# The normaliser sums of an mLSTM block with the keys as the moving operand, in column groups of TensorE

## The reference, cut to what matters

```python
def step(carry, inp):                       # _mlstm_chunked, float32
    C, n, m = carry
    ...
    wsL = jnp.exp(bL[..., None] - b + ib - m_new[..., None])
    wpL = jnp.exp(bL + m - m_new)
    C_new = wpL[..., None, None] * C + jnp.einsum('bhs,bhsv,bhsd->bhvd', wsL, vb, kb)
    n_new = wpL[..., None] * n + jnp.einsum('bhs,bhsd->bhd', wsL, kb)
    return (C_new, n_new, m_new), h
```

## Time and profile before

| | |
|---|---|
| runs, median (lowest to highest) | 2135.77 us (2133.35 to 2139.61) |
| the profiled execution, its own time | 2138.1 us |
| its span | 2136.3 us |
| TensorE busy | 2047.6 us, 96% |
| VectorE, ScalarE, GpSimd busy | 49%, 20%, 42% |
| mean granted TensorE clock | 0.979 of full |
| moved by DMA | 224.49 MB, 105 GB/s |

### The profile page before, as it was taken

How to read it: one execution, slowest core, us unless ns; L and a number is a source line. 1 busy time by engine, 2 the same in 40 slices (tenths; PEclk the granted TensorE clock), 3 DMA queues, 4 the chain that set the end, 5 groups by cost and what they waited for, 6 DMA issues and landing times.

```text
span 2136.3 us, 33690 instructions
## 1 busy us (share of the span) xinstructions
PE 2047.6 (96%) x13453; PEld 1871.6 (88%) x13453; DVE 1047.9 (49%) x1230; ACT 428.8 (20%) x671; POOL 895.3 (42%) x568
## 2 busy tenths in 40 slices
PE   6999999899999999989999999999899999999997
PEld 5989988799999999989998746547499999999996
DVE  4655646554415414576962356555732441442345
ACT  3232333321101100131212323323211110010011
POOL 4323333145445445554553123223445444544543
PEclk9999999899999999999999999999999999999998
DMA  4122212122222222233232474756732222222222
GB/s 174 60 70 78 85 54 91 42 69 70 78 79 70 79 79 70 88 108 127 79 103 77 144 259 146 275 191 208 282 104 74 71 76 79 69 79 72 76 79 89
DMA packets 82080, 224.49 MB, mean 105 GB/s; under 512 B 6352, under 2 KB 11344, under 8 KB 81232
## 3 DMA queue, kind: packets, MB, share of 16 engines
q1 hardware_dynamic: 73344, 202.94, 28.7%
q10 hardware_dynamic: 8656, 20.39, 2.6%
HBM read 170.06 MB, written 53.25 MB: 105 GB/s over the span
## 4 chain that ended last, share of the span: by engine, by line
PE 85%; DVE 8%; DMA 3%; ACT 2%; issue 1%; POOL 1%; DVEq 0%; SPq 0%; ACTq 0%; POOLq 0%
PE psd L211 12%; PE psd L216 11%; PE psd L212 11%; PE psd L215 11%; PE psd L217 11%; PE psd L218 11%; PE psm L429 2%; PE psm L1397 1%; PE psd L1293 1%; DMA c_s<-CsB 1%; PE psd L1282 1%; PE psd L1219 1%; DMA CsB<-st_c 1%; PE psm L1382 1%; DVE ntmp L306 1%
## 5 line engine op out<-in xcount | busy, mean ns | idle before, releaser
L1986 POOL CAST whi<-wraw 128x1024 fp32r<-128x1024 f32 x223 | 236.7, 1062 | 935.2 <-PE psd L218 501.9
L1988 POOL TENSOR_TENSOR wlo<-wraw,whi 128x1024 fp32r<-128x1024 f32 x223 | 543.9, 2439 | 17.9
L211 PE MATMUL psd<-xh,whi 128*128 128x320 f32 x896 | 286.3, 320 | 9.6 <-ACT xh L269 3.5
L215 PE MATMUL psd<-xl,whi 128*128 128x320 f32 x896 | 279.6, 312 | 2.7 <-POOL xl L324 2.2
L211 PE MATMUL psd<-ah,whi 128*128 128x320 f32 x864 | 269.2, 312 | 12.1 <-DVE ffs L974 7.7
L212 PE MATMUL psd<-xh,whi 128*128 128x320 f32 x896 | 278.8, 311 | 0.0
L216 PE MATMUL psd<-xl,whi 128*128 128x320 f32 x896 | 278.7, 311 | 0.0
L218 PE MATMUL psd<-xh,wlo 128*128 128x320 f32 x896 | 278.6, 311 | 0.0
L217 PE MATMUL psd<-xh,wlo 128*128 128x320 f32 x896 | 278.6, 311 | 0.0
L212 PE MATMUL psd<-ah,whi 128*128 128x320 f32 x864 | 267.9, 310 | 0.0
L216 PE MATMUL psd<-al,whi 128*128 128x320 f32 x864 | 267.8, 310 | 0.0
(11 more groups left out here) (396 smaller groups left out, 3225.2 us busy)
## 6 DMA issues: line engine op xcount, KB each, us to landing
wraw<-w SPq DMA_DIRECT2D x224, 512.0 KB, 3.5
CsA<-st_c SPq DMA_DIRECT2D x7, 1024.0 KB, 6.3
CsB<-st_c SPq DMA_DIRECT2D x7, 1024.0 KB, 9.1
c_s<-CsA SPq DMA_DIRECT2D x7, 1024.0 KB, 6.5
c_s<-CsB SPq DMA_DIRECT2D x7, 1024.0 KB, 9.4
ztp<-st_c SPq DMA_DIRECT2D x5, 1024.0 KB, 8.4
CsC<-st_c SPq DMA_DIRECT2D x5, 1024.0 KB, 9.4
c_s<-ztp SPq DMA_DIRECT2D x5, 1024.0 KB, 4.2
```

The costliest lines, as they stand in the source:

```text
L211: pe.matmul(o0, wh, x0, start=st, stop=False)
L215: pe.matmul(o0, wh, l0, start=False, stop=False)
L1986: pool.tensor_copy(whi[s][:], wraw[s][:]).then_inc(w_high, 1)
L1988: pool.tensor_tensor(wlo[s][:], wraw[s][:], whi[s][:].bitcast(F32), ALU.subtract).then_inc(w_split, 1)
```

## The change

For each head the sums are made in three steps. First, in column groups: for each of the four prompt tiles one product with a 128x32 block `n_one` as the stationary operand (a column of ones, the rest zeros) and the tile of keys, 512 columns, as the moving one; the four write to four groups of 32 partitions of bank 1, so that partitions 0, 32, 64 and 96 hold the four partial sums. A fifth product with `n_smp` (columns 1 to 8 pick the streams) adds the streams' sums to partitions 1 to 8. They are issued ahead of the products L1377 and L1379. Second, ScalarE copies the bank to a new tile `nrow` (step "nr"). Third, after L1377 and L1379, four products take 128 columns of `nrow` each as the stationary operand and 16 columns `n_sum` as the moving one, which turns the sums onto the partitions of the key and adds the four partial sums up. VectorE reads them at a stride of 16 columns. The three constants are put in places of the parameter tile that the convolution has used up, by four more operations of `fold`, for which the gate products wait.

```diff
+        NW = 16
+        n_one, n_smp = [par[:, PAR["convw"] + GW * i:PAR["convw"] + GW * (i + 1)] for i in range(2)]
+        n_sum = par[:, PAR["convb"]:PAR["convb"] + NW]
...
+        nrow = sb("nrow", [P, SEQ], at=x3)
...
-                                  + {0: ["nu"], 2: ["sum", ("upd", 0)], 4: [("upd", 1)], 6: ["var", ("upd", 2)],
+                                  + {0: ["nr", "nu"], 2: ["sum", ("upd", 0)], 4: [("upd", 1)], 6: ["var", ("upd", 2)],
...
-                               + [("num", f) for f in kts] + ["dn", "dnS", "D", "DS", ("Cp", 0)]
+                               + [("num", f) for f in kts] + ["dn", "nr", "dnS", "D", "DS", ("Cp", 0)]
...
+                link(v.memset(par[:, PAR["convw"]:PAR["convw"] + 2 * GW], 0.0))
+                link(v.memset(n_one[:, 0:1], 1.0))
+                link(v.tensor_copy(n_smp[:, 1:1 + NB], con[:, CON["ind"]:CON["ind"] + NB]))
+                link(v.tensor_copy(n_sum, gsel[:, 0:NW]))
...
-                pe.wait_ge(self.gw, 30)
+                pe.wait_ge(self.gw, 34)
...
             def pe_normalisers(self, pe, h):
 
                 P_, V_, S_ = self.P, self.V, self.S
+                for c in range(NP):
+                    mm = pe.matmul(bank[1][GW * c:GW * (c + 1), :], n_one, ktok[:, c, :], start=True, stop=c > 0,
+                                   skip_group_check=True)
+                mm = pe.matmul(bank[1][0:GW, :], n_smp, ktok[:, NP, :], start=False, stop=True, skip_group_check=True)
+                mm.then_inc(P_.sem, 1)
                 pe.wait_ge(V_.sem, V_.at("qn", h))
                 pe.matmul(bank[0][:, 0:P], ones, att[:, tt(NP)], start=True, stop=False)
                 for k in range(KH):
                     pe.matmul(bank[0][:, 0:P], ones, rt[:, k, :], start=False, stop=(k == KH - 1))
+                pe.wait_ge(S_.sem, S_.at("nr", h))
                 for k in range(KH):
-                    for c in range(NP):
-                        pe.matmul(bank[0][:, P + k:P + k + 1], ktok[:, c, tt(k)], ones[:, 0:1], start=(c == 0),
-                                  stop=(c == NP - 1))
-                    mm = pe.matmul(bank[0][:, 2 * P + NB * k:2 * P + NB * (k + 1)], ktok[:, NP, tt(k)],
-                                   con[:, CON["ind"]:CON["ind"] + NB], start=True, stop=True)
+                    mm = pe.matmul(bank[0][:, P + NW * k:P + NW * (k + 1)], nrow[:, tt(k)], n_sum, start=False,
+                                   stop=(k == KH - 1), skip_group_check=True)
                 mm.then_inc(P_.sem, 1)
...
-                    v.tensor_copy(nP[:, h, :], bank[0][:, P:P + KH]).then_inc(V_.sem, 1)
+                    both = bank[0][:, P:P + NW * KH].rearrange("p (k b) -> p k b", b=NW)
+                    v.tensor_copy(nP[:, h, :].unsqueeze(2), both[:, :, 0:1]).then_inc(V_.sem, 1)
                     v.wait_ge(V_.sem, V_.at("nsd", h))
-                    v.tensor_tensor(ns, ns, bank[0][:, 2 * P:2 * P + KH * NB].rearrange("p (k b) -> p k b", b=NB), ALU.add)\
+                    v.tensor_tensor(ns, ns, both[:, :, 1:1 + NB], ALU.add)\
                         .then_inc(V_.sem, 1)
...
                 a.activation(att[:, 0:SEQ], B[0], ACT.Abs).then_inc(S_.sem, 1)
+                a.wait_ge(P_.sem, P_.at("nr", h))
+                a.activation(nrow[:], bank[1], ACT.Copy).then_inc(S_.sem, 1)
                 if h:
                     self.act_hi_s(a, h - 1)
```

## The result

The changed kernel takes 2118.86 us (median of four runs, 2117.91 to 2121.25) beside 2137.69 us of the kernel before (four runs, 2133.35 to 2141.08). The ratio is 0.9914, 95% interval 0.9902 to 0.9926: 18.8 us faster, where 19.8 were forecast. The profiled execution took 2117.95 us (span 2116.2), 20.15 less than the profiled one of before.

What follows compares the result with a forecast made beforehand. TensorE, 85% of the chain, bounds the kernel. Per head 11.66 - (2.71 + 3.99) = 4.96 us, four heads 19.8: profiled 2138.1 to 2118.3, or 2116.0 from the median 2135.8; range 2111 to 2130.

Steps and rivals of the forecast that it cites:

- Products: Sums step on TensorE: column groups 1.00, fifth product 0.86, turning products 0.85, 2.71 us in place of 4.88 per head.
- The cost of entering the column mode: Column groups on TensorE: a set following other work costs 1.00 us, one following its like 0.88; entering costs about 0.12.
- the 0.5 that I set next to the sum: Leaving the column mode for the streams' denominators may cost about 0.12 again, making the sum 0.5 us worse over four heads.
- Clock: TensorE after the sums step: no fall to half clock expected, so unit 1 takes 3.99 us, 2.79 less in head 0.
- My other argument against that rule: Against blaming idle gaps for clock falls: after 2.40 us of TensorE waiting for CsB, the clock was still 1.00.
- Copy: ScalarE's 0.60 us copy out of PSUM, hidden behind 1.22 us of streams' denominators; uncovered, some 0.7 us per head.
- I had moved GpSimd's sums later by 4.0 us: GpSimd's three sums queue behind L1662, pushed 4.0 us later; in head 1 they end at 1318.1 and stay covered.
- Enough, by 0.2 to 0.3 us: VectorE's four updates of unit 1 end at 4.7 us after "nu"; TensorE wants them for unit 2 at 4.98.
- The wait at unit 7: TensorE's wait for CsB before unit 7's read, expected still to be 2 to 3 us.
- second rival: Unit 7: the gain turns into a longer wait for CsB, three heads gain nothing, one 5.0 us: 2130.8; chance 0.07.
- nothing older is in its way: Argument against a longer CsB wait: the store waits for VectorE's updates alone; DMA share before unit 2 is 0.00.

Runs made afterwards that it cites:

- wide_ones: Kernel before, with 88 columns of ones in place of one as the moving operand of the 64 products L1382: 2128.30 us, ratio 0.9958.
- sums_behind: Changed kernel with the streams' denominators issued first and the column products behind them, so nothing covers ScalarE's copy: 2127.83 us, ratio 0.9955.
- copy_last: Changed kernel with ScalarE's copy of the sums behind the copy for the head before and the next head's inputs: 2126.22 us, ratio 0.9948.
- nine kernels counted above: The kernel before, the changed kernel and seven experiments, in which stores of CsB were counted over heads 0 to 2; no single time.
- sums_in_wait: Changed kernel with the column products ahead of unit 7's read and the turning products behind it, instead of in unit 0: 2117.28 us, ratio 0.9908.

## Why the prediction was right, and where a size was off

- **Products.** 0.88 + 0.96 + 0.90 = 2.74 us, predicted 1.00 + 0.86 + 0.85 = 2.71. The cost of entering the column mode that I took from the reads did not show: 0.88 here, behind products in row groups. Leaving it may: the fifth took 0.96, not 0.86. So the drain that the Trainium skill speaks of ("TensorEngine Tiling (Array Packing)", section "Key Properties") cost at most 0.1 us per head, 0.4 in four, beside the 0.5 that I set next to the sum.
- **Clock.** Unit 1 takes 3.98 us in all heads, predicted 3.99; wide_ones shows that the thin products were the cause, and with wider ones the kernel before gains 9 us. The rule of the Trainium skill that lays falls to gaps in which TensorE idles ("TensorE: Matmul & The Clock Gate", section "HAM oscillation — how this bites in real kernels") does not cover this fall: no gap preceded it (TensorE was busy 3.10 of 3.10 us, rows 3). My other argument against that rule, a stretch of 2.40 us in which TensorE stood and no fall came, was one case: in the later kernels most waits of 2 us and more were followed by one (counted in the last section).
- **Copy.** Hidden, as said; sums_behind shows the 0.7 us that it costs without cover.
- **GpSimd and VectorE: mis-sized.** "Enough, by 0.2 to 0.3 us" had VectorE's denominators at head 0's 0.89 us. I had moved GpSimd's sums later by 4.0 us, and looked only at the product that waits for them, not at what runs beside them. In heads 1 to 3 the denominators took 2.93 us, and unit 2 1.2 longer, 3.6 in all. copy_last shows it: with the sums out of the way both are back.
- **The wait at unit 7: mis-sized.** I kept it at 2 to 3 us in each head, and my second rival had it grow. It was 2.02, 1.62 and 0: 3.7 us came back, 3.3 of them in heads 1 and 2, where the delayed unit 2 moved a store away from a load. That the forecast of 19.8 came out near 18.5 for the heads owes something to luck: the 3.6 us lost in unit 2 and the 3.7 won at unit 7 cancel. The second rival's "nothing older is in its way" looked at the stretch before unit 2 and overlooked the load of CsA, which SyncE issues 0.87 us ahead of the store in the kernel before too:

```profile
1242.75 0.38 SPq L1752 DMA_DIRECT2D CsA<-st_c  x1
1243.62 0.37 SPq L1757 DMA_DIRECT2D c_s<-CsB  x1
```

- **Not foreseen:** a fall of the clock after head 0's wait, 1.6 us.

## What to carry to other kernels

Read the granted clock behind every stretch of thin products, not only in it: here their successor paid more than they did. When an edit moves work of one engine, list what then runs beside it on the engine that shares its memory port, with durations from a head in which the two meet. And before shortening a stretch that ends in a wait for a transfer, see what that transfer shares its time with: 1.2 us less on TensorE in each of three heads cost 7 us, until two lines of the transfer order were exchanged.

## What the runs showed of the hardware that was not expected

- The clock fell with TensorE busy without a gap: behind 16 one-column products (32 instructions) under weight loads, and behind 8 of them (2.2 us). With 88 columns at the same pace of instructions it did not.
- In the nine kernels counted above, sums_in_wait left out, waits for CsB of 1.9 to 3.7 us were followed by a mean clock of 0.50 to 0.69 over the next 4 us in 15 heads (1.5 to 2.9 us lost in each), and six of 1.6 to 2.75 us by 1.00, among them the three of the kernel before. The length alone does not separate them; what does stays open.
- VectorE's 128x512 and 128x128 operations with two SBUF inputs took 1.65 and 1.35 us beside GpSimd's additions, 0.68 and 0.28 alone.
- A 1 MB store took 5.2 to 5.6 us when it was issued ahead of a 1 MB load, 5.8 to 6.7 when the load had been issued 1.5 to 1.8 us earlier, and 7.5 to 9.3 when that was 0.4 to 1.2 us earlier.
